# Six groups of 432 columns in a projection, and another order of gathers, loads and row sums in an expert-output stage

## The reference, cut to what matters

```python
proj = h @ w_in                               # (T,1024) @ (1024,3600)
z, xbc, dt_raw, rq, rk, rv, rg = split(proj, [512, 1536, 1552, 2064, 2576, 3088])
xbc = silu(depthwise_conv_centred(xbc, conv_w, conv_b))   # 5 taps over tokens, 1024 channels
...                                           # two scans, output projection, gated residual
# PEER: 8 heads x 16 picks = 128 experts of 16384 for each token
act = gelu(einsum('tkd,td->tk', u_tab[ix], hx))
y   = einsum('tk,tkd->td', gx * act, v_tab[ix])
y_out = rmsnorm(x + g2 * y, lnf_w)
```

## Time and profile before

| | us |
|---|---|
| median of three timed runs | 3724.32 |
| the profiled execution's own time | 3714.26 |
| its span, first to last instruction | 3712.6 |
| PE busy | 3380.9 |
| DVE busy | 2838.1 |
| POOL busy | 1754.5 |
| ACT busy | 1253.6 |

### The profile page before, as it was taken

How to read it: one execution, slowest core, us unless ns; L and a number is a source line. 1 busy time by engine, 2 the same in 40 slices (tenths; PEclk the granted TensorE clock), 3 DMA queues, 4 the chain that set the end, 5 groups by cost and what they waited for, 6 DMA issues and landing times. The chain is left out here.

```text
span 3712.6 us, 50329 instructions
## 1 busy us (share of the span) xinstructions
PE 3380.9 (91%) x17854; PEld 2992.1 (81%) x17854; DVE 2838.1 (76%) x4693; ACT 1253.6 (34%) x2291; POOL 1754.5 (47%) x1014
## 2 busy tenths in 40 slices
PE   5999969599799999999898899996999999999998
PEld 2998859554799999999888888896777777778786
DVE  4544337497577899999899999954888888888887
ACT  2321125233323222222677777731212212212221
POOL 0000012121111487787788888874655565565530
PEclk8979979799899999999999999998999999999999
DMA  5225424542111578777889898887999999999993
GB/s 183 95 77 168 135 85 156 164 145 85 52 35 47 171 241 270 241 257 250 292 332 342 326 342 343 337 322 279 337 313 343 324 323 332 328 312 336 329 314 122
DMA packets 379343, 880.17 MB, mean 237 GB/s; under 512 B 33554, under 2 KB 192962, under 8 KB 376018
## 3 DMA queue, kind: packets, MB, share of 16 engines
q1 hardware_dynamic: 255876, 390.51, 32.4%
q0 software_dynamic: 116064, 423.24, 31.5%
q10 hardware_dynamic: 7280, 65.01, 4.5%
HBM read 740.54 MB, written 138.11 MB: 237 GB/s over the span
## 5 line engine op out<-in xcount | busy, mean ns | idle before, releaser
L1861 POOL DMA_INDIRECT hT<-peer_v,hT x336 | 571.5, 1701 | 450.9 <-DVE hrow L1882 367.8
L1725 PE MATMUL ps<-h_hi,u_hi 128*128 128x384 f32 x2048 | 699.9, 342 | 30.3 <-POOL u_lo L1611 22.5
L1725 PE MATMUL ps<-h_hi,u_lo 128*128 128x384 f32 x2048 | 690.2, 337 | 0.0
L1725 PE MATMUL ps<-h_lo,u_hi 128*128 128x384 f32 x2048 | 690.1, 337 | 0.0
L1985 PE MATMUL ps<-v_hi,a_hi 128*128 128x512 f32 x1536 | 607.0, 395 | 66.9 <-DVE acc L1910 36.2
L1985 PE MATMUL ps<-vw_rest,a_hi 128*128 128x512 f32 x1536 | 604.4, 393 | 0.0
L1985 PE MATMUL ps<-v_hi,ga_rest 128*128 128x512 f32 x1536 | 603.9, 393 | 0.0
L1607 POOL DMA_INDIRECT hT<-u_rows,hT x224 | 376.6, 1681 | 95.7 <-issue 51.6
L1882 DVE SCALAR_TENSOR_TENSOR hrow<-hT,dots,hrow 128x1024 f32<-128x1024 f32 x336 | 418.1, 1276 | 0.0
L1725 PEld LDWEIGHTS ps<-h_hi,u_hi 128*128 128x128 f32 x2048 | 389.6, 190 | 33.9 <-issue 29.6
L1611 POOL TENSOR_TENSOR u_lo<-uw,u_hi 128x1024 fp32r<-128x1024 f32 x126 | 340.1, 2699 | 157.8 <-ACT u_hi L1518 155.3
(11 more groups left out here) (338 smaller groups left out, 5889.8 us busy)
## 6 DMA issues: line engine op xcount, KB each, us to landing
uw<-u_T SPq DMA_DIRECT2D x128, 512.0 KB
vw<-peer_v SPq DMA_DIRECT2D x128, 512.0 KB, 11.6
s_d<-so SPq DMA_DIRECT2D x256, 192.0 KB
gates_d<-big ACTq DMA_DIRECT2D x24, 2048.0 KB
gt<-gates_d SPq DMA_DIRECT2D x32, 1536.0 KB
ga<-s_d SPq DMA_DIRECT2D x128, 384.0 KB, 12.1
wmr<-w_modT SPq DMA_DIRECT2D x32, 512.0 KB
tok_d<-st SPq DMA_DIRECT2D x45, 256.0 KB, 2.2
```

The lines of the kernel that those rows point to most:

```text
L1725: mm = pe.matmul(g.ps[4 + 2 * s + b][:, 0:HALF], u[s][:, k, :], h[:, k, b * HALF:(b + 1) * HALF], start=(k == 0 and i == 0), stop=(k == KD ...
L1861: pool.indirect_dma_start(rows[n % NU], None, g.v_rows, bass.IndirectOffsetOnAxis(ap=g.pick[m % GT][:, m // GT:m // GT + 1], axis=0)).then ...
```

## The change

In the projection the 16 dt columns are appended to the other token-row columns, with 16 columns of zeros, to 2592 = 6 x 432 columns. The weights come in two arrays laid out for it (`w_xbc`, `w_tok`), the dt matmuls, their split and their store go, ACT copies three tiles of the first group before the last SiLU, and PE waits for one block's copy less before the groups. In the outputs SP waits for the second v slice of the first block before it issues the second block's gates and loads, POOL waits for the fifth gating before its first gather, and DVE's order is another. SHARE gives the row sets that stand at four places of a block.

```diff
-TC = PROJ - XBC
+TW = 432
+TC = 6 * TW
...
-            pe.wait_ge(wd_lo_ready, 1)
-            for t in range(NT):
-                rows = slice(t * P, (t + 1) * P)
-                for k in range(KD):
-                    for m, (h, w) in enumerate(((h_hi, wd_hi), (h_hi, wd_lo), (g.hT_lo, wd_hi))):
-                        mm = pe.matmul(g.ps[6][:, 16 * t:16 * t + 16], h[:, k, rows], w[:, k, :],
-                                       start=(k == 0 and m == 0), stop=(k == KD - 1 and m == 2))
-            mm.then_inc(dt_done, 1)
-            pe.wait_ge(banks_free, NB + 2)
+            pe.wait_ge(banks_free, NB + 1)
...
-                            mm = pe.matmul(g.ps[t % NQ][:], h[:, k, rows], w[s][:, k, :],
+                            mm = pe.matmul(g.ps[t % NQ][:, 0:TW], h[:, k, rows], w[s][:, k, :],
...
+            group(0, range(NQ))
             silu(NB - 1, 1, NB // 2 - 1)
...
-VO = GT * NSEL - V1
-STEPS = 6 + 7 * 28
+SHARE = (2, 3, 5, 2)
+STEPS = sum(SHARE) * 28
...
-            for j in range(2):
-                gates(j, j)
-                loads(j, j)
+            gates(0, 0)
+            loads(0, 0)
+            sp.wait_ge(v_loaded[1], 16)
+            gates(1, 1)
+            loads(1, 1)
...
         def _(pool):
+            pool.wait_ge(a_ready, BL + 1)
             for n in range(VO):
...
-            for e in range(BL + 2):
+            for e in range(BL + 1):
                 gated(e)
-                step = rows_between(step)
-            for j in range(NB - 2):
+            for j in range(NB - 1):
                 for t in range(TR):
                     take(j, t)
-                    if j == NB - 3:
-                        finish_first(t)
-                    step = rows_between(step)
-                    for e in ((BL * (j + 1) + 2 + t,) if t < 2 else (BL * (j + 2), BL * (j + 2) + 1)):
-                        gated(e)
-                        step = rows_between(step)
-            dve.sem_inc(ms_ready, 1)
-            for t in range(TR):
-                take(NB - 2, t)
-                if t < 2:
-                    gated(NE - 2 + t)
+                    if j == NB - 3 and t == TR - 1:
+                        for q in range(GT):
+                            finish_first(q)
+                    for e in ((1,), (2, 3), ())[t]:
+                        gated(BL * (j + 1) + e)
+                    step = rows_between(step, SHARE[t])
+                if j < NB - 2:
+                    gated(BL * (j + 2))
+                    step = rows_between(step, SHARE[3])
+                if j == NB - 3:
+                    dve.sem_inc(ms_ready, 1)
...
-        "w_in": A["w_in"][0],
+        "w_xbc": f(A["w_in"][0][:, 512:512 + XBC]),
+        "w_tok": f(np.concatenate([A["w_in"][0][:, 0:512], A["w_in"][0][:, REST0:], A["w_in"][0][:, 512 + XBC:REST0],
+                                   np.zeros((D, TC - (PROJ - XBC)), np.float32)], 1)),
```

More of the change, by code:

```diff
@@ L299, in project_in @@
     NQ = 3
+    NG = TC // TW
     with ExitStack() as ctx:
@@ L319, in project_in @@
         cv_stored = [sem("cvst0"), sem("cvst1")]
-        dt_done, dt_copied, dt_stored = sem("dt"), sem("dtcopied"), sem("dtstored")
         tile_done, tile_copied, group_done = sem("tile"), sem("tilecopied"), sem("group")
         st_stored = [sem(f"st{i}") for i in range(NQ)]
-        wv = g.w_in.rearrange("(k p) n -> p k n", p=P)
+        wv, tv = (w.rearrange("(k p) n -> p k n", p=P) for w in (g.w_xbc, g.w_tok))
         wm, cb2 = [sb(f"wmr{i}", [P, D]) for i in range(2)], sb("cboth", [P, 2, D])
@@ L338, in groups @@
             body(0, 0)
-            with eng.Fori(0, 2) as i:
+            body(1, 1)
+            with eng.Fori(1, NG // 2) as i:
+                body(i * 2, 0)
                 body(i * 2 + 1, 1)
-                body(i * 2 + 2, 0)
         @block.gpsimd
@@ L350, in _ @@
             for s in range(2):
[L351 to L354, removed]
+                pool.dma_start(wx[s][:], wv[:, :, s * P:(s + 1) * P]).then_inc(wx_loaded[s], 16)
+            for j in range(2):
+                pool.dma_start(wt[j][:], tv[:, :, j * TW:(j + 1) * TW]).then_inc(wt_loaded[j], 16)
             with pool.Fori(0, NB // 2 - 1) as i:
@@ L357, in _ @@
                     pool.wait_ge(block_done, i * 2 + s + 1)
[L358 to L362, removed]
+                    pool.dma_start(wx[s][:], wv[:, :, bass.ds(i * (2 * P) + (2 + s) * P, P)]).then_inc(wx_loaded[s], 16)
+            for j in range(2, NG):
+                pool.wait_ge(group_done, j - 1)
+                pool.dma_start(wt[j % 2][:], tv[:, :, j * TW:(j + 1) * TW]).then_inc(wt_loaded[j % 2], 16)
         @block.sync
@@ L386, in _ @@
             load_mod(1)
-            for grp in range(5):
+            for grp in range(NG):
                 for t in range(NT):
@@ L431, in group @@
                     rows = slice(t * P, (t + 1) * P)
-                    if not (isinstance(grp, int) and t < NQ):
+                    if not (isinstance(grp, int) and grp * NT + t < NQ):
                         pe.wait_ge(tile_copied, grp * NT + (t - NQ + 1))
@@ L497, in _, with group @@
             split_t(1)
+            def group(grp, tiles):
+                for t in tiles:
+                    act.wait_ge(tile_done, grp * NT + t + 1)
+                    act.wait_ge(st_stored[t % NQ], grp * (16 * NT // NQ) + (t // NQ) * 16 + 16)
+                    act.activation(st[t % NQ][:], g.ps[t % NQ][:, 0:TW], ACT.Copy).then_inc(tile_copied, 1)
+            group(0, range(NQ))
             silu(NB - 1, 1, NB // 2 - 1)
@@ L500, in _ @@
             act.activation(cb2[:], cb2[:], ACT.Silu).then_inc(mod_silu, 1)
[L501 to L511, removed]
+            for grp in range(NG):
+                group(grp, range(NQ if grp == 0 else 0, NT))
+                if grp + 2 < NG:
                     split_t(grp + 2)
@@ L1846, in _ @@
                     ready(m * RING + s, s, m)
-            for s in range(RING - 2):
+            for s in range(RING - 3):
                 ready(NE - RING + s, s, NE // RING - 1)
             root(0)
-            for s in range(RING - 2, RING):
+            for s in range(RING - 3, RING):
                 ready(NE - RING + s, s, NE // RING - 1)
@@ L1882, in add_row, with rows_between @@
                 dve.scalar_tensor_tensor(g.hrow[:, q], rows[n % NU], g.dots[:, q, i:i + 1], g.hrow[:, q], ALU.mult, ALU.add).then_inc(added, 1)
-            def rows_between(step):
-                for n in range(min(VO * step // STEPS, VO), min(VO * (step + 1) // STEPS, VO)):
+            def rows_between(step, many):
+                for n in range(min(VO * step // STEPS, VO), min(VO * (step + many) // STEPS, VO)):
                     add_row(n)
-                return step + 1
+                return step + many
             def gated(e):
```

30 lines of the change are left out of this document (10 added, 20 removed).

## The result

The changed kernel takes 3630.2 us (median of 4 runs, 3625.4 to 3631.4), the kernel before 3725.6 beside it (3722.5 to 3728.4): a ratio of 0.9742, with an interval of 0.9726 to 0.9757. Forecast were 3643 and 3622 to 3682. The profiled executions took 3714.3 and 3630.7 us (spans 3712.6 and 3628.9), mean granted clock 0.960 and 0.968.

| stretch | before | after | change | forecast |
|---|---|---|---|---|
| start to the end of the projection's groups | 490.8 | 466.1 | -24.7 | -29.4 |
| end of the groups to the outputs' first v load | 2077.5 | 2078.9 | +1.4 | 0 |
| that load's issue to the outputs' first matmul | 26.1 | 15.9 | -10.2 | -10 |
| matmuls of the outputs | 1103.2 | 1053.0 | -50.2 | -41.7 |
| after the last matmul | 15.0 | 14.9 | -0.1 | 0 |

A forecast was written before the change was run, and what follows sets the result against it. PE was taken as bound, losing 55.7 us in the outputs' steady part to waits and lower clock. Projection -29.4 and outputs -51.7 made -81, from 3724.3 to 3643; own range 3625 to 3655, with rivals 3622 to 3682.

The forecast's parts named there:

- The dt matmuls: Projection: 216 matmuls of 16 columns, all on PE's path, go: -42.3 us.
- the columns: Projection: 45 tiles of 5.49 us become 54 of 4.66 us, 247.2 to 251.7: +4.5 us.
- The wait on the first weights: Projection: the split of the first weights, hidden before by the dt matmuls, now makes PE wait 4.6 us.
- Store slots: Projection: slots come free late, so PE's third reuse of a bank can wait: +3 us, bounds 0 and 10.7.
- Turns: Projection: turns of six groups and a fresh start at the lower clock take 5.5 us instead of 4.7: +0.8.
- Loads: Projection: loads from `w_xbc` and `w_tok`, same bytes per block, other row pitch: 0 us, bounds -3 and +5.
- The start: Outputs: fewer bytes ahead of the first gating, which comes at about 2580: -10 us, bounds 0 and -13.
- The steady part: Outputs: DVE's new order removes 55.7 us of stalls; late loads cost 10 us back, bounds 0 and 120.
- L: Outputs: time from a block's first load issue to DVE's first gating of it; 6.4 to 10.2 us before.
- The point of 10.7: Outputs: the L from which PE stalls with DVE's new order, moved from 6.6 in the old order.
- rivals A and C: Outputs' steady part: A, gathers push L to about 11.6, 3669, chance 0.15; C, L of 13, 3753, chance 0.04.
- The tail: Outputs' end: `finish_first` for three tiles, 11 us, delays block 31's first gating, so PE waits: +4 us with the clock.

The follow-up runs named there:

- the second execution: Profiled execution of the changed kernel run once more, unchanged; span 3617.5 us, timed 3626.7 us, ratio 0.9739.
- the other shares: Changed kernel with row-set shares 4, 5, 1, 2 instead of 2, 3, 5, 2, one row ahead of the next gating; 3624.9 us, ratio 0.9752.
- the run with two gatings: Changed kernel with two gatings ahead of a block's first sum, as before, five rows kept; 3633.2 us, ratio 0.9767.

## Why the prediction was right, and which step failed

The forecast was the right case, its time 13 us high. By its own terms:

*The dt matmuls (-42.3) and the columns (+4.5)*: a tile takes 4.68 us (forecast 4.66), 54 of them 252.7, so +5.5. *The wait on the first weights*: 4.61 measured, 4.6 forecast. *Store slots*: 4.0 us of waits for `st` where 3 were taken, of a bound of 10.7; the later full reloads did not stop PE. *Turns*: from 202.87 to 466.11 it is 263.2 us, less 252.7 for tiles and 4.0 for slots leaves 6.5, where 5.5 were taken and 4.7 stood before: +1.8. *Loads*: PE is through with the xbc blocks 1.6 us later than before in this execution, where 0 was taken. That is no cost of the change as far as the traces show: the second execution's first xbc matmul is 4.2 us earlier, and from first to last start these matmuls take 105.4 and 106.1 us, against 106.3 before. The sum -42.3 + 5.5 + 4.6 + 4.0 + 1.8 + 1.6 is -24.8, against -24.7 measured. Four terms were 1 to 2 us short each, all on the same side.

*The start*: -10.2, forecast -10. The bytes ahead of the first gating were the right cause, and the run without POOL's wait shows that it was the gathers, which delay both SP's issue and the landing.

*The steady part, the step that failed*: "L of 9.5 to 10.5 ... I take 10 us over 28 blocks". All of the old loss went and nothing came back. From the third block to the last but one L is at most 7.6 in the changed kernel, where DVE's own five row sets hold the gating, and 6.0 to 6.6 where the arrival can be seen. The point of 10.7 was never put to the test, and rivals A and C had nothing to start from. So the 55.7 us went with two things at once, a later point and earlier arrivals, and no run has one without the other. By the prediction's numbers each would have been enough: no L of before (at most 10.2) reaches 10.7, and arrivals of 6.0 to 6.6 do not pass the old point of 6.6.

I had taken the number of gathers near the load issue for the cause. By itself it isn't: gathers end at 0.0, 1.2, 3.6, 4.8, 6.1 and 7.3 us after the issue in the changed kernel, at 0.0, 1.2, 2.5, 3.7 and 6.0 with the other shares, and in the block of the earlier trace rows that had L = 9.2 at 0.0, 1.2, 3.5 and 4.8 too. Nearly the same gathers, another L. What differs is what the DMA engines deliver behind the issue. First the block of before (issue at 2985.43), then the changed kernel (issue at 2866.04); the last three columns are the granted clock, the busy share of the DMA engines and GB/s:

```profile
2985.00:2987.00 2.00, 2.00 (x11) 1.65 (x10) 2.00 (x4) 0.00 (x0) 1.39 (x3) 1.00 0.77 260
2987.00:2989.00 2.00, 2.00 (x11) 1.65 (x10) 1.14 (x1) 0.00 (x0) 1.96 (x1) 1.00 0.78 246
2989.00:2991.00 2.00, 2.00 (x11) 1.65 (x10) 0.00 (x0) 0.00 (x0) 0.94 (x1) 1.00 0.98 326
```

```profile
2865.00:2867.00 2.00, 2.00 (x10) 1.65 (x9) 2.00 (x4) 0.00 (x0) 1.70 (x2) 1.00 0.34 32
2867.00:2869.00 2.00, 2.00 (x11) 1.65 (x10) 2.00 (x4) 0.00 (x0) 1.70 (x2) 1.00 0.78 291
2869.00:2871.00 2.00, 2.00 (x11) 1.65 (x10) 2.00 (x2) 0.29 (x1) 1.57 (x2) 1.00 1.02 413
```

The first v slice is split 6.7 us after the issue there and 4.66 here. Over the 8 blocks of before with an L over 9.1 the rate from 1.5 to 5 us behind the issue is 264 to 317 GB/s; in the changed kernel, over the 12 blocks from 2637.6 to 2996.6, it is 369 to 407. The total alone does not tell: in the block of the earlier trace rows with L = 6.4 (issue at 3022.90) it is 278, but there next to no gather is in flight and the loads have it to themselves. By queue it is plainer. Here are the 4 us from 2 us behind the same two issues (2987.43 to 2991.43 before, 2868.04 to 2872.04 now), with packets, MB and share of the 16 engines; q1 are SP's loads, q0 POOL's gathers:

```profile
q1 hardware_dynamic: 189, 0.67, 50.2%
q0 software_dynamic: 141, 0.52, 41.1%
```

```profile
q1 hardware_dynamic: 324, 1.07, 66.1%
q0 software_dynamic: 158, 0.58, 36.4%
```

The gathers move no more than in the changed kernel; it is the loads that move less, and a packet of theirs takes 0.17 us of an engine instead of 0.13 (the share of 16 times 4 us, divided by the packets). So in all 8 blocks: 165 to 212 GB/s for the loads, against 258 to 278.

Seven of these 8 have one gather more, which ends 1.2 us ahead of the issue. It is one that took 4.6 us of POOL, and three more follow it in a row:

```profile
2979.56 4.62 POOL L1861 DMA_INDIRECT hT<-peer_v,hT  x1 [1.45 <-DVE hrow L1882]
```

In the changed kernel no gather of the outputs takes over 2.1 us of POOL. That could be why; but one more block of before has the same gathers and an L of 8.6, the eighth has an L of 9.9 without them, and in the run with two gatings gathers end 2.9, 1.6 and 0.4 us ahead of the issue, and L is 7.6 at most. Why a packet takes longer there stays open. A run that moves one gather to 1.2 us ahead of the issue would tell; it wasn't tried.

I was also wrong to take 365 GB/s for the fullest rate: the changed kernel moves 407 over the 20 us from 2869, and before already had 403 over the 3 us from 2978. By the round robin of the Trainium skill ("DMA: Bandwidth & Descriptors", section "Queues, rings and completion order") the steady part would lose nothing. It lost nothing, and L stayed below the 8.9 that I had worked out by it. But the 9.2 to 10.2 us of before are above that bound, although there too the loads get more than half of what is moved (0.67 of 1.19 MB above). The bound took the full rate for granted, and that is what was missing, so the rule alone does not give L.

*The tail*: forecast were 2.4 us for `acc`, about 1 for the last kept, and the clock, +4. Measured are 2.43 and 1.18. The matmuls' 1053.0 us are 8.5 over the 1044.5 without a stall; with the 3 us that the prediction has at the start, about 5.5 are left for the tail (an estimate), where 4 were taken. The granted clock is 0.50 (1.2 GHz) in the 2 us from 3567.3 and 1.00 (2.4 GHz) again from 3571.3.

*Profiled and timed*: the sum was set against the median of three runs, +10 us. The stages outside the change vary by nearly as much (8.6 us between the two executions of the changed kernel). By the profiled execution's own time -81 stands against -83.5 measured, and that agreement is partly luck, with -24.7 for -29.4 and -50.2 for -41.7.

## What to carry to other kernels

Where an engine's order sets a stall, write down the arrival time from which it stalls and the slack of the engine, and choose an order with this point past every arrival seen. Here the whole loss went with such an order, and the exact place of the filler work mattered little. Arrival times of loads are not to be carried over from a stalling pattern to one that does not stall: here they fell by about 3 us without a byte less, so that the later point may not have been needed. When a transfer waits at the start of a stage, look for the gathers that another queue put ahead of it before anything else.

## What the runs showed of the hardware

- Matmuls with 128x128 weights start 0.2267 us apart at 512 columns (outputs), 0.195 at 432, 0.1734 at 384 and 0.148 at 324, close to a straight line. Going on down it, 16 columns would be 0.02 (an estimate from these four); the 216 of them took 0.196 each. They start 0.11 apart at first, and then the granted clock falls to the lower level (1.2 GHz) though PE is busy all the time, and stays there to their end, with 0.21 from start to start. At 0.11 all of them would be 24 us (an estimate), so of the 42.3 us that the change took away some 18 were the lower clock. From the kernel before; after the busy times come the granted clock, DMA share, GB/s:

```profile
198.00:200.00 2.00, 2.00 (x21) 2.00 (x20) 1.69 (x1) 0.28 (x1) 0.00 (x0) 1.00 0.00 0
...
210.00:230.00 20.00, 20.00 (x95) 20.00 (x95) 10.85 (x6) 8.33 (x9) 0.00 (x0) 0.50 0.09 35
```
- Loads with rows of 3 and 4 KB and gathers together moved 407 GB/s over 20 us on one core, at a DMA share of 1.03 (changed kernel, 2869 to 2889 us).
- Eight gathers issued ahead of a load doubled the time from its issue to its use, from 6.8 to 13.5 us, and held SP's issue of another for 4 us more.
- The length of a wait of PE does not tell by itself whether the lower clock follows. In the changed kernel it followed the wait of 2.43 us in the tail (0.50 behind 3567.3), and it did not follow the wait of 2.43 us in the groups (1.00 behind 236.0) nor the one of 1.18 us. In the second execution it did follow the wait of 2.12 us at the same place of the groups (0.50 behind 232.5).
